# Layer 1's second feed-forward product by seven block products per chunk in place of eight, with the sums of blocks on VectorE

## What is computed

```
D_MODEL, SEQ, D_FF = 1024, 512, 4096

def channel_mixer(a, w1, w2):
    return jnp.square(jax.nn.relu(a @ w1)) @ w2

f = channel_mixer(modulate(rms_norm(h, g[2]), mod[3], mod[4]), w_ff1[layer], w_ff2[layer])
h = h + mod[5] * rms_norm(f, g[3])
```

## Time and profile before

| | |
|---|---|
| median of 3 runs | 1687.67 us (1686.56 to 1688.31) |
| the profiled execution | 1686.46 us |
| its span, first to last instruction | 1684.7 us |
| mean granted TensorE clock | 0.998 |
| busy: TensorE, VectorE, ScalarE, GpSimd | 97%, 64%, 40%, 9% |

### The profile page before, as it was taken

How to read it: one execution, slowest core, us unless ns; L and a number is a source line. 1 busy time by engine, 2 the same in 40 slices (tenths; PEclk the granted TensorE clock), 3 DMA queues, 4 the chain that set the end, 5 groups by cost and what they waited for, 6 DMA issues and landing times.

```text
span 1684.7 us, 25555 instructions
## 1 busy us (share of the span) xinstructions
PE 1636.6 (97%) x9788; PEld 1421.5 (84%) x9788; DVE 1082.8 (64%) x1912; ACT 672.0 (40%) x1265; POOL 157.7 (9%) x171
## 2 busy tenths in 40 slices
PE   6999999999999999999999999999999899999997
PEld 4999888778889989899899877988878788888886
DVE  5889787683666675665666787826785644444446
ACT  5433467774553122122122156416674632222221
POOL 1000265231000000000000000003440000000000
PEclk9999999999999999999999999999999999999999
DMA  8533430013122342433423302203023122222221
GB/s 342 185 122 137 124 86 20 20 51 126 50 76 95 130 150 101 150 125 124 143 106 116 150 33 100 76 0 101 17 86 125 51 100 100 97 86 92 100 100 50
DMA packets 30254, 170.31 MB, mean 101 GB/s; under 512 B 3920, under 2 KB 6864, under 8 KB 12112
## 3 DMA queue, kind: packets, MB, share of 16 engines
q1 hardware_dynamic: 30160, 169.03, 28.5%
HBM read 156.17 MB, written 2.10 MB: 94 GB/s over the span
## 4 chain that ended last, share of the span: by engine, by line
PE 84%; DVE 8%; DMA 2%; ACT 2%; issue 2%; SPq 1%; POOL 0%; DVEq 0%; ACTq 0%
PE ps L1251 25%; PE ps L997 14%; PE ps L998 14%; PE ps L999 14%; PE ps L1049 3%; PE ps L1170 2%; PE ps L1143 2%; PE ps L1063 2%; DMA first_raw<-in_w_ada 2%; PE ps L1083 1%; PE ps L1121 1%; PE ps L1078 1%; PE ps L1131 1%; DVE nmax L2748 1%; ACT junk L1658 1%
## 5 line engine op out<-in xcount | busy, mean ns | idle before, releaser
L1627 ACT ACTIVATE whi<-raw 128x2048 fp32r<-128x2048 f32 x78 | 149.0, 1910 | 314.3 <-PE ps L999 287.6
L997 PE MATMUL ps<-whi,uhi 128*128 128x512 f32 x640 | 249.9, 390 | 0.2 <-DVE wlo L2255 0.2
L999 PE MATMUL ps<-whi,ulo 128*128 128x512 f32 x640 | 249.1, 389 | 0.0
L998 PE MATMUL ps<-wlo,uhi 128*128 128x512 f32 x640 | 249.1, 389 | 0.0
L2255 DVE TENSOR_TENSOR wlo<-raw,whi 128x2048 fp32r<-128x2048 f32 x78 | 178.7, 2290 | 88.9 <-ACT whi L1627 88.6
L1251 PE MATMUL ps<-ahi,whi 128*128 128x384 f32 (+1 forms) x720 | 215.3, 353 | 1.1 <-ACT relu L2094 1.1
L1251 PE MATMUL ps<-alo,whi 128*128 128x384 f32 (+1 forms) x720 | 215.2, 352 | 0.0
L1251 PE MATMUL ps<-ahi,wlo 128*128 128x384 f32 (+1 forms) x720 | 215.2, 352 | 0.0
L2681 DVE SCALAR_TENSOR_TENSOR ada_junk<-raw,silu_rows 128x1024 bf16<-128x1024 f32 x160 | 195.5, 1222 | 25.8 <-DMA raw<-in_w_ada_t 23.2
L997 PE MATMUL ps<-whi,ahi 128*128 128x256 f32 (+1 forms) x512 | 155.7, 304 | 3.5 <-DVE alo L3065 1.6
L999 PE MATMUL ps<-whi,alo 128*128 128x256 f32 (+1 forms) x512 | 153.4, 300 | 0.0
(11 more groups left out here) (265 smaller groups left out, 2857.7 us busy)
## 6 DMA issues: line engine op xcount, KB each, us to landing
raw<-in_w_ff SPq DMA_DIRECT2D x64, 1024.0 KB, 4.8
raw<-in_w_ada_t SPq DMA_DIRECT2D x40, 1024.0 KB, 4.8
raw<-in_w_in_odd SPq DMA_DIRECT2D x9, 1024.0 KB, 4.8
first_raw<-in_w_ada SPq DMA_DIRECT2D x8, 1024.0 KB, 21.3
raw<-in_w_in_even SPq DMA_DIRECT2D x8, 1024.0 KB, 4.8
h<-in_x SPq DMA_DIRECT2D x4, 1024.0 KB, 7.1
raw<-in_w_out_even SPq DMA_DIRECT2D x4, 1024.0 KB, 6.6
raw<-in_na_bias SPq DMA_DIRECT2D x4, 1024.0 KB, 5.1
```

The lines of the kernel that those rows point to most:

```text
L997: pe.matmul(dst, lhs[0], rhs[0], start=first, stop=False)
L998: pe.matmul(dst, lhs[0], rhs[1], start=False, stop=False)
L999: return pe.matmul(dst, lhs[1], rhs[0], start=False, stop=last)
L1627: act.activation(whi[w % 2][:, :, :], raw[r % 2][:, :, :], ACT.Copy).then_inc(s_hi, 1)
```

## The change

TensorE and SyncE (cut):

```diff
+            def ff_by_blocks(r0, w0):
+
+                def load(kind, c, half):
+                    r = (up_raw if kind == 1 else down_raw)(c, half)
+                    src = (w_ff1 if kind == 1 else w_ff2)[1][2 * c + half]
+                    sp.dma_start(raw[r % 2][:, :, :].rearrange("p k n -> p (k n)"), src).then_inc(s_raw[r % 2], 16)
+
+                def blocks_taken(c, half):
+                    sp.wait_ge(s_blo, weight_count(c, ("b21", "b22")[half]))
+                    sp.wait_ge(s_wsum, 4 * c + (4, 3)[half])
+
+                for half in range(2):
+                    sp.wait_ge(s_lo, w0 - 1 + half)
+                    load(1, 0, half)
+                for c in range(1, 8):
+                    for half in range(2):
+                        if c == 1:
+                            sp.wait_ge(s_lo, w0 + half + 1)
+                        else:
+                            blocks_taken(c - 2, half)
+                        load(1, c, half)
+                    for half in range(2):
+                        sp.wait_ge(s_lo, w0 + 2 * c + half + 1)
+                        load(2, c - 1, half)
+                for half in range(2):
+                    blocks_taken(6, half)
+                    load(2, 7, half)
...
+                def product(c, j):
+
+                    pe.wait_ge(s_vlo, token_count(c, TOKEN_BLOCKS[j]))
+                    pe.wait_ge(s_blo, weight_count(c, WEIGHT_BLOCKS[j]))
+                    slot = (7 * c + j) % 4
+                    for t in range(2):
+                        g = F2_LAST + 14 * c + 2 * j + t
+                        if g - F2_LAST >= 4:
+                            pe.wait_ge(s_f2f, g - 3)
+                        a = slice(P * t, P * t + P)
+                        for k in range(2):
+                            last = three_pass(bank(g % 4), (token_hi[j][:, k, a], token_lo[j][:, k, a]),
+                                              (ring_hi[slot][:, k, :], ring_lo[slot][:, k, :]), k == 0, k == 1)
+                        last.then_inc(s_f2, 1)
...
+                for c in range(7):
+                    hidden(c + 1, 0)
+                    product(c, 0)
+                    product(c, 1)
+                    hidden(c + 1, 1)
+                    product(c, 2)
+                    product(c, 3)
+                    hidden(c + 1, 2)
+                    product(c, 4)
+                    product(c, 5)
+                    hidden(c + 1, 3)
+                    product(c, 6)
+                pe.wait_ge(s_relu, F1_LAST + 32)
+                last_down()
```

VectorE's takings and its list for the last chunk but one (the whole order of a chunk shows in the excerpts below; its helpers do one subtraction or addition each):

```diff
+                def take(c, j):
+                    g = F2_LAST + 14 * c + 2 * j
+                    dve.wait_ge(s_f2, g + 2)
+                    src = ps[:, 512 * (g % 4):512 * (g % 4) + 1024].rearrange("p (t n) -> p t n", t=2)
+                    dst = product_sum(SEVEN[j])
+                    if c == 0:
+                        dve.tensor_copy(dst, src).then_inc(s_f2f, 2)
+                    else:
+                        dve.wait_ge(s_f2f, g - 12)
+                        dve.tensor_tensor(dst, dst, src, ALU.add).then_inc(s_f2f, 2)
+
+                def combine(dst, x, y, op, after):
+                    dve.wait_ge(s_comb, after)
+                    dve.tensor_tensor(product_sum(dst), product_sum(x), product_sum(y), op).then_inc(s_comb, 1)
...
+                dve.wait_ge(s_f2f, product_end(6, 5))
+                combine(2, 2, 1, ALU.add, 0)
+                combine(6, 6, 1, ALU.add, 0)
+                combine(3, 3, 6, ALU.add, 2)
+                combine(7, 7, 6, ALU.add, 2)
+                combine(3, 3, 5, ALU.add, 3)
+                combine(5, 5, 7, ALU.add, 4)
+                token_part(7, "a12")
+                token_part(7, "a22")
+                take(6, 6)
+                weight_part(7, "b12")
+                weight_part(7, "b22")
+                dve.wait_ge(s_f2f, product_end(6, 6))
+                combine(4, 7, 4, ALU.subtract, 4)
+                dve.wait_ge(s_f1, F1_LAST + 32)
+                gate_diagonals("gate11", 1, 1)
```

ScalarE's list:

```diff
+                for c in range(-1, 7):
+                    if c >= 0:
+                        up_hi(c + 1, 1)
+                        hidden(c, 3)
+                        for name in ("a12", "a22", "s1", "s2", "s4"):
+                            token_part(c, name)
+                    hidden(c + 1, 0)
+                    if c >= 0:
+                        for name in ("b22", "t3", "t1", "t2"):
+                            weight_part(c, name)
+                    hidden(c + 1, 1)
+                    token_part(c + 1, "a11")
+                    if c >= 0:
+                        weight_part(c, "t4")
+                    token_part(c + 1, "s3" if c < 6 else "a21")
+                    if c < 6:
+                        up_hi(c + 2, 0)
+                    hidden(c + 1, 2)
+                    weight_part(c + 1, "b11")
+                    weight_part(c + 1, "b21")
+                hidden(7, 3)
+                token_part(7, "a12")
+                token_part(7, "a22")
+                weight_part(7, "b12")
+                weight_part(7, "b22")
+                for half in range(2):
+                    copy_group(("gate11", 0, half))
+                ff_boundary(1, F2_LAST + 98)
```

More of the change, by code:

```diff
@@ L322, in build @@
         s_f2f = sem("down_added")
+        s_bhi = sem("weight_block_hi_done")
+        s_blo = sem("weight_block_lo_done")
+        s_wsum = sem("weight_blocks_summed")
+        s_vhi = sem("token_block_hi_done")
+        s_vlo = sem("token_block_lo_done")
+        s_vsum = sem("token_blocks_summed")
+        s_comb = sem("product_sums_combined")
         s_mx = sem("max_done")
@@ L991, in gate_rows @@
                         wait_group_copied(pe, n - 4)
-                        pe.matmul(bank(4 + n % 4), ones, diag[:, 2 * s + half, :, :].rearrange("p a b -> p (a b)"),
+                        rows_ = diag_last if tag == "gate11" else diag
+                        pe.matmul(bank(4 + n % 4), ones, rows_[:, 2 * s + half, :, :].rearrange("p a b -> p (a b)"),
                                   start=True, stop=True).then_inc(s_tg, 1)
@@ L1210, in product_tile, with first_hidden, product @@
                 last.then_inc(s_g, 1)
+            def first_hidden(layer, w):
+                tag = f"pre{layer}1"
+                def product(k, s):
+                    wait_weights(w, k)
+                    a = norm_span(tag, s)
+                    hi, lo = weight_parts(w)
+                    for mt in range(2):
+                        c0 = 512 * (4 + 2 * mt) + a.start
+                        last = three_pass(ps[:, c0:c0 + a.stop - a.start],
+                                          (hi[:, k, P * mt:P * mt + P], lo[:, k, P * mt:P * mt + P]),
+                                          (ahi[:, k, a], alo[:, k, a]), k == 0, k == KT - 1)
+                        if s == 1 and k == KT - 1:
+                            last.then_inc(s_f1, 1)
+                norm_phase(tag, product)
@@ L1216, in ff @@
                 f2_base = 0 if layer == 0 else 8 * 2 * NT
[L1218 to L1234, removed]
                 def hidden(c_par, wpos, wdyn, m0, mdyn, first=False):
@@ L1291, in ff @@
                 per = 2 * nt
-                first_hidden(w0)
+                first_hidden(layer, w0)
                 hidden(0, w0, 0, f1_base, 0, first=True)
@@ L2573, in gate_diagonals @@
                         col = gcol[:, layer, sub, 4 * half:4 * half + 4, s]
[L2574 removed]
+                        rows_ = diag_last if tag == "gate11" else diag
+                        dve.tensor_tensor(rows_[:, 2 * s + half, :, :], ident.unsqueeze(1).broadcast_to([P, 4, P]),
                                           col.unsqueeze(2).broadcast_to([P, 4, P]), ALU.mult).then_inc(s_dg, 1)
```

246 lines of the change are left out of this document (228 added, 18 removed).

## The result

The changed kernel takes **1675.1 us** (median of 4 runs, 1674.47 to 1676.97), the kernel before 1687.16 us in the same comparison (1686.56 to 1688.31): a ratio of 0.993, with a 95% interval of 0.9912 to 0.9947. That is 12.1 us less. The forecast was 1675.7 us. The profiled execution took 1674.72 us with a span of 1672.9, where that of before had 1686.46 and 1684.7; it was forecast at 1674.5.

The account below looks back on a forecast made before the run. TensorE was taken as the bound: -19.04 us for matmuls removed, +2.8 in the first chunk, +4.2 at the end of chunk 6, sum -12.0. Profiled 1686.46 becomes 1674.5; with the median 1.2 above, 1675.7 us, range 1672.8 to 1683.0.

Parts of the forecast that it names:

- What bounds the kernel: Layer 1's feed-forward chunks: TensorE busy throughout, 192 matmuls in 43.52 us, so matmuls removed shorten the time.
- the matmuls removed (-19.04 us): First seven chunks: down product falls from 96 to 84 matmuls at 0.2267 us each, saving 19.04 us.
- VectorE and ScalarE added: Per chunk, VectorE rises from 19.9 to 34.1 us, ScalarE from 12.4 to 20.6; TensorE's 40.8 us leaves VectorE at 84%.
- The rule of no overlap: Each VectorE instruction waits for the previous one's pipe flush; by it the saving would be 11.0 us, time 1676.7.
- A steady chunk, 2.4 us spare: VectorE's chain takes product 1 at 16.6 us, product 3 needs its banks at 19.04; no wait, 40.8 us per chunk.
- The first chunk: Chunk 0: late second up unit split costs TensorE 2.2 us in three pieces before products 1, 2 and 3; 2.8 taken.
- The allowance of 0.6: Chunk 0: loss taken as 2.8 us, the middle between 2.2 walked and 3.4 if no VectorE instructions overlapped.
- The end of chunk 6: Before the last chunk: six accumulator sums on VectorE delay the tokens; TensorE waits 3.9 us, taken as 4.2.
- The clock (rival 1, chance 0.27): Behind the wait at the end of chunk 6: clock falls, one 12-matmul group at half pace costs 2.7 us; 1678.4; chance 0.27.
- Chain without spare: Steady chunks: 0.17 us more per VectorE instruction makes the chain 0.7 us late in six chunks; 1684 us; chance 0.11.
- VectorE as the bound: Seven chunks: 0.35 us more per VectorE instruction makes each 3.9 us late, 27 us in all; 1703 us; chance 0.06.

Follow-up runs that it names:

- two more sums: Changed kernel with two more 1024-element subtractions on VectorE ahead of the first sum of weight blocks in chunks 1 to 6; 1676.80 us.
- Tokens first: Changed kernel with four of seven accumulator sums at the end of chunk 6 moved behind the last token and weight blocks on VectorE; 1670.68 us.
- four further sums: Changed kernel with four more 1024-element subtractions on VectorE ahead of the first sum of weight blocks in chunks 1 to 6; 1692.77 us.
- all three edits: Changed kernel with Tokens first, chunk 1's second up unit split before b11 and b21 of chunk 0, and chunk 7's a22 in s1's place; 1670.37 us.
- 96 matmuls: Changed kernel with product 6 accumulated twice in chunks 0 to 5, output no longer the reference's; 1692.28 us.

## Why the prediction was right, point by point

- **What bounds the kernel; the matmuls removed (-19.04 us).** Right: 40.80 us per chunk, TensorE busy for all of it, and putting 12 matmuls per chunk back costs what they were priced at.
- **VectorE and ScalarE added.** Right. The forms that no row had, 1024 elements taken from two banks and the sums of 1024, measure 1217 to 1226 ns against the 1.22 us taken. (Its 84% adds up lengths; the 79% of the windows counts overlaps once.) On VectorE's timeline an instruction starts 0.09 us before the one ahead has ended (1444.27 + 1.22 to 1445.41, with two more sums), and 0.03 behind that end where it waits for a semaphore of the one ahead (1445.41 + 1.22 to 1446.66). The rule of no overlap in the Trainium skill ("VectorE: DVE Perf Modes", Terms), which the prediction weighed, is thus not what this trace shows for the first kind; by it the time would have been 1676.7.
- **A steady chunk, 2.4 us spare.** Right in place and nearly in size: 2.2 measured. The chain reaches product 1 at 16.6 us as walked (from the remainder at 1428.92 to 1444.79 + 1.22 = 1446.01 in the changed kernel it is 17.1 us, and the remainder starts 0.5 ahead of the hidden block), as these rows show at its two ends.

```profile
1428.92 2.29 DVE L3247 TENSOR_TENSOR wlo<-raw,whi 128x2048 fp32r<-128x2048 f32 x1 [3.90 <-ACT whi L2297]
...
1444.79 1.22 DVE L3313 TENSOR_TENSOR xn<-xn,ps 128x1024 f32<-128x1024 f32 x1
```

- **The first chunk.** Mechanism right, size off. I walked 2.2 us in three pieces and took 2.8; it lost 1.47 in two, before products 2 and 3. The remainder of the second up unit started at 5.07 instead of 5.5 us, so that product 1 was taken 0.8 us sooner. The allowance of 0.6 for pairs that don't overlap wasn't needed, since the overlap holds nearly all along the list.
- **The end of chunk 6.** Right: 3.83 us against 3.9 walked; the 4.2 that I took had an allowance for the same reason. Tokens first shows that sums ahead of the tokens are its cause: moving three of the six took 2.1 us of it, until ScalarE's copies were what the tokens waited for.
- **The clock (rival 1, chance 0.27).** This step of the forecast failed: I made its likeliest case the one without a fall, and the fall came in both profiles of the changed kernel, at 1.7 us instead of the rival's 2.7. That the number came within 0.6 us is luck: this 1.7 and the two allowances that were too large, 1.3 and 0.4, cancel. The rival's own sum, 2.7 on top of both allowances, was 3.3 us too high.
- **Chain without spare, VectorE as the bound.** Neither happened. The last two of four further sums show what it would have taken: beyond the spare, 2.51 us more in VectorE's list made every chunk 2.52 us longer.

## What to carry to other kernels

Before work is moved from the engine that is the bound to one that executes in strict order, walk that engine's list against the times at which each result is wanted; its busy share (79% here, 85% where it already set the pace) doesn't tell whether the trade pays. Look at the first and the last turn of the loop apart: the steady turns cost nothing, and all that was given back (5.3 us of waits and 1.7 of clock, out of 19) lay in those two, where three lines moved got 3.7 us back. And price an idle stretch of TensorE at its own length plus the matmuls that may run at half pace behind it.

## What the runs showed of the hardware

- Where the granted clock falls differs between executions. TensorE waits 1.93 us at about 1309 to 1311 us in all eleven profiles of this study, the one of before included; the clock fell there in 2 of them, and within or just behind a later wait of 1.7 us, at 1323 to 1325 us, in 5 others, and at neither place in 4. The waits of 3.7 us at the end of chunk 6 had a fall in or just behind them in all 6 profiles that kept them idle; those of 0.7 to 1.6 us there had none.
- The fall came 3.8 us behind the end of TensorE's last matmul in the changed kernel (1633.44 to about 1637.28, from the window's mean of 0.64), and 2.2 us behind it at 1311 us with all three edits and at the end of chunk 6 with two more sums. With 96 matmuls it came 4.5 us behind it at the end of chunk 6, when TensorE had been at work again for 0.6 us. It lasted 3.4 us in all these places but one, 6.8 with two more sums.
- A fall at 1311 us delays the start of the part by 1.6 us (26.0 us from there to the start with all three edits, 24.4 in the changed kernel), one at 1323 to 1325 us by 0.5 to 0.7. The first is most of why the part began 1.4 us later with 96 matmuls than in the changed kernel, and 1.9 later with all three edits than with tokens first: a difference of 2 us between two single executions tells nothing here until the clock has been looked at.
- Three engines read and write the same weight tiles in a steady chunk at 27% of the DMA time, and no instruction was slower for it: matmuls 0.2267 us apart, 2048 elements on VectorE 2.293 us, as in the earlier trace rows.
